# Projection tiles 4 to 27 in pairs, by seven block products in place of eight

## The reference, cut to what matters

```
u = h @ w_in                                   # 320 x 1024 @ 1024 x 14640, fp32
u_gate, u_gla, u_rwkv, u_ssm = _split(u, (N_GATE, GLA_PROJ, RWKV_PROJ, SSM_PROJ))
# RWKV rows are mixed with the row before them:
us = u + (full[:, :-1] - u) * mu
```

## Time and profile before

| what | value |
|---|---|
| median of 3 runs | 1505.06 us (1503.83 to 1506.8) |
| span of the profiled execution | 1502.1 us |
| PE busy | 1457.5 us, 97% |
| PEld busy | 1011.2 us, 67% |
| DVE, ACT, POOL busy | 647.1, 390.4, 116.8 us |
| granted TensorE clock, mean | 0.996 |

### The profile page before, as it was taken

The page is one execution under the profiler, slowest core; times in us unless marked ns, Lnnn a source line. Parts: engine busy times, 40 slices in busy tenths (PEclk is TensorE's granted clock), DMA queues, the critical chain, the costliest instruction groups (busy, mean ns, idle before and its releaser), DMA issues.

```text
span 1502.1 us, 31068 instructions
## 1 busy us (share of the span) xinstructions
PE 1457.5 (97%) x13071; PEld 1011.2 (67%) x13071; DVE 647.1 (43%) x1227; ACT 390.4 (26%) x874; POOL 116.8 (8%) x107
## 2 busy tenths in 40 slices
PE   7999999999999999999999999999999999999995
PEld 6776667677776777767766765766666767675751
DVE  5223778875644677734541114622211112121228
ACT  2112444442322554435431011111111111111111
POOL 3000113121010000000000000000000001000000
PEclk9999999999999999999999999999999999999998
DMA  7778375563344544565577538689999999999985
GB/s 243 168 174 181 101 214 166 132 203 97 103 130 147 138 112 116 178 180 163 135 231 263 157 100 359 251 337 399 417 423 430 428 426 429 426 428 429 427 342 211
DMA packets 157017, 375.27 MB, mean 250 GB/s; under 512 B 101708, under 2 KB 110300, under 8 KB 139216
## 3 DMA queue, kind: packets, MB, share of 16 engines
q1 hardware_dynamic: 123712, 341.35, 63.9%
q10 hardware_dynamic: 26592, 15.49, 3.5%
q0 software_dynamic: 6576, 16.48, 3.2%
HBM read 327.14 MB, written 51.95 MB: 252 GB/s over the span
## 4 chain that ended last, share of the span: by engine, by line
PE 82%; DVE 7%; DMA 4%; ACT 2%; DVEq 2%; issue 1%; SPq 1%; ACTq 1%; POOLq 0%
PE PS L576 27%; PE PS L1069 14%; PE PS L919 8%; PE PS L1036 7%; PE PS L1088 6%; PE PS L624 4%; PE PS L1041 2%; PE PS L957 2%; DVE region L1492 2%; DVE region L1499 2%; PE PS L632 1%; ACT L1172 1%; PE PS L1052 1%; PE PS L1077 1%; PE PS L817 1%
## 5 line engine op out<-in xcount | busy, mean ns | idle before, releaser
L576 PE MATMUL PS<-h0T,region 128*128 128x320 f32 x1808 | 510.2, 437 | 1.0 <-issue 0.8
L576 PEld LDWEIGHTS PS<-h0T,region 128*128 128x128 f32 x1808 | 336.8, 190 | 144.6 <-issue 12.2
L1172 ACT ACTIVATE region<-PS 128x9 f32<-128x9 f32 (+6 forms) x407 | 148.5, 383 | 681.9 <-PE PS L576 311.8
L1069 PE MATMUL PS<-region 128*64 128x512 f32 x1024 | 228.8, 592 | 0.0
L1069 PEld LDWEIGHTS PS<-region 128*64 128x64 f32 x1024 | 124.5, 137 | 92.2 <-issue 31.9
L1492 DVE TENSOR_TENSOR region<-region 128x256 f32<-128x256 f32 (+10 forms) x210 | 127.0, 624 | 96.8 <-ACTq L1218 76.2
L919 PE MATMUL PS<-region 128*128 128x320 f32 x512 | 138.6, 433 | 1.3 <-DMA region<-wo 1.2
L919 PEld LDWEIGHTS PS<-region 128*128 128x128 f32 x512 | 97.0, 190 | 42.5 <-issue 1.7
L1172 ACT ACT_TABLE_LOAD x80 | 102.6, 1283 | 73.1 <-DMA region<-projected 56.7
L1088 PE MATMUL PS<-region,history 128*64 128x512 f32 x512 | 119.7, 596 | 1.0 <-ACTq L1454 0.7
L1172 ACT ACTIVATE region<-region 128x256 f32<-128x256 f32 (+8 forms) x160 | 81.2, 531 | 147.9 <-DMA region<-projected 37.0
(11 more groups left out here) (210 smaller groups left out, 1163.8 us busy)
## 6 DMA issues: line engine op xcount, KB each, us to landing
region<-moe_w SPq DMA_DIRECT2D x64, 2048.0 KB, 17.4
region<-moe_w SPq DMA_DIRECT2D x64, 1024.0 KB, 15.0
region<-w_in SPq DMA_DIRECT2D x115, 512.0 KB, 5.6
region<-wo SPq DMA_DIRECT2D x32, 512.0 KB, 3.6
projected<-region ACTq DMA_DIRECT2D x65, 167.5 KB, 3.9
expert_rows<-region SPq DMA_DIRECT2D x20, 512.0 KB, 7.2
region<-expert_rows SPq DMA_DIRECT2D x5, 2048.0 KB, 14.4
region<-projected SPq DMA_DIRECT2D x10, 768.0 KB, 6.3
```

What stands on the lines that cost most here:

```text
L576: last = mm(PS[:, 6 + i % 2, 0:NTOK], WR[:, i, k, :], H0T[:, k, :], start=(k == 0), stop=(k == KT - 1))
L1069: last = mm(PS[tiles(i), 2, :], XE[:, k, tiles(i)], W13[r][i][:, k * 512:k * 512 + 512], start=(k == 0), stop=(k == KT - 1))
L1172: return nc.scalar.activation(out, in_, f, **kw)
```

## The change

Tiles 4 to 27 are computed two at a time. Two tiles are 256 features by 320 tokens over a width of 1024, which is cut into 2 x 2 x 2 blocks: feature tile a or b, the first or second half of the width (four blocks of 128 each), and the first or second 32 tokens of each chunk (`H0H[:, k, 0]` and `H0H[:, k, 1]`, 160 tokens each). Eight block products would be needed; the scheme takes seven, each of four matmuls with 160 moving columns, on sums and differences of blocks. Three PSUM banks (`X`, `Z`, `W`) hold them, two sets of three by turns.

- DVE makes four differences of token blocks once (`TSUM`), each 128 x 640, and adds the partial sums in PSUM onto staged parts, four `TENSOR_TENSOR` of 160 columns for a pair (`quads`).
- POOL makes four sums of weight blocks for every pair (`weight_sums`), each a `TENSOR_TENSOR` of 128 x 512, and one sixth of its old job after each of the pairs 1 to 6 (`keep_rows`).
- ACT copies four partial sums out of PSUM for a pair (`keep`), then the chunk edges (`edges`), and issues the stores of the pair before between its second and third `keep` (`tile_out`).
- PE signals `tile_done` for both tiles in its fifth product, since the last two products read only sums.
- SP's wait for `h_kept` goes; the scale and bias have moved. Three semaphores are shared under double names.

```diff
+            def project_pair(m, u):
+                pair, a, b = m * 2 + u - 2, 2 * u, 2 * u + 1
+                X, Z, W = (quad_sum(3 * u + x) for x in range(3))
+                def product(out, lhs, rhs, start, freed=False):
+                    for k in range(KH):
+                        last = mm(out, lhs(k), rhs(k), start=start and k == 0, stop=k == KH - 1, skip_group_check=True)
+                        if freed and k < 2:
+                            last.then_inc(sem("tile_done"), 1)
+                    last.then_inc(sem("quad"), 1)
+                for i in (a, b):
+                    pe.wait_ge(sem(f"weights_in{i}"), (m + 1) * 16)
+                pe.wait_ge(sem("quads_out"), pair + 1)
+                product(X, lambda k: WR[:, a, k, :], lambda k: H0H[:, k, 0], True)
+                product(Z, lambda k: WR[:, b, KH + k, :], lambda k: TSUM[:, 3, k], True)
+                pe.wait_ge(sem("weights_summed"), pair + 1)
+                pe.wait_ge(sem("quad_kept"), pair * 4 + 1)
+                product(X, lambda k: WSUM[u][:, 1, k], lambda k: TSUM[:, 1, k], False)
+                pe.wait_ge(sem("quad_kept"), pair * 4 + 2)
+                product(Z, lambda k: WR[:, a, KH + k, :], lambda k: H0H[:, KH + k, 0], True)
+                product(W, lambda k: WSUM[u][:, 0, k], lambda k: TSUM[:, 0, k], True, True)
+                pe.wait_ge(sem("quad_kept"), pair * 4 + 3)
+                product(X, lambda k: WSUM[u][:, 2, k], lambda k: TSUM[:, 2, k], False)
+                pe.wait_ge(sem("quad_kept"), pair * 4 + 4)
+                product(W, lambda k: WSUM[u][:, 3, k], lambda k: H0H[:, KH + k, 1], False)
...
+            pe.wait_ge(sem("token_sums"), 1)
             with pe.Fori(1, PRE // RING) as m:
-                for i in range(RING):
-                    project(m, i)
+                for u in range(2):
+                    project_pair(m, u)
...
+            for p in range(PAIRS):
...
+                act.wait_ge(sem("tile_mixed"), 2 * p + 2)
+                keep(p, 1, a, 0, X)
+                keep(p, 2, b, 0, Z)
+                if p > 0:
+                    for n in (RING + 2 * p - 2, RING + 2 * p - 1):
+                        tile_out(n)
+                keep(p, 3, a, 1, X)
+                keep(p, 5, b, 1, W)
+                act.wait_ge(sem("quads_out"), p + 3)
+                for n in (RING + 2 * p, RING + 2 * p + 1):
+                    edges(n)
+                act.drain().then_inc(sem("tile_moved"), 2)
...
+            def quads(p):
...
+                dve.wait_ge(sem("quad"), 7 * p + 4)
+                dve.wait_ge(sem("quad_kept"), 4 * p + 1)
+                tt(quad_out(a, 0), quad_out(a, 0), Z, add)
+                dve.wait_ge(sem("quad"), 7 * p + 6)
+                dve.wait_ge(sem("quad_kept"), 4 * p + 4)
+                for j in range(2):
+                    tt(quad_out(b, j), quad_out(b, j), X, add)
+                dve.wait_ge(sem("quad"), 7 * p + 7)
+                tt(quad_out(a, 1), quad_out(a, 1), W, add)
+                dve.drain().then_inc(sem("quads_out"), 1)
...
+            def weight_sums(p):
...
+                for i in (a, b):
+                    pool.wait_ge(sem(f"weights_in{i}"), (p // 2 + 2) * 16)
+                if p > 1:
+                    pool.wait_ge(sem("quad"), 7 * p - 7)
+                ptt(S1, A21, A22, add)
+                ptt(S3, A11, A21, sub)
                 pool.drain()
+                ptt(S2, S1, A11, sub)
+                pool.drain()
+                ptt(S4, A12, S2, sub)
+                pool.drain().then_inc(sem("weights_summed"), 1)
```

More of the change, by code:

```diff
@@ L175, in hybrid_layer, with quad_sum, quad_out @@
         assert at[0] <= REGION.shape[1], at[0]
+        tail = REGION[:, at[0]:at[0] + 2048]
+        assert at[0] + 2048 <= REGION.shape[1]
         LORA, G2 = (OT[:, 16:].rearrange("p a b -> p (a b)")[:, k * D:k * D + D] for k in range(2))
+        TSUM = shaped(OT[:, 8:16].rearrange("p a b -> p (a b)"), 4, KT // 2, NTOK // 2)
+        spare = OT[:, 16:].rearrange("p a b -> p (a b)")[:, 2 * D:]
+        WSUM = [shaped(v, 4, KT // 2, 128) for v in (spare[:, 0:2048], tail)]
+        H0H = H0T.rearrange("p k (c h w) -> p k h c w", c=NCH, h=2)
+        KH = KT // 2
+        def quad_sum(b):
+            return shaped(PS[:, b, 0:NTOK // 2], NCH, L // 2)
+        def quad_out(i, j):
+            return STG[:, i, :, HIST + 32 * j:HIST + 32 * j + 32]
         at[0] = mixer_base
@@ L1226, in move, with keep, edges @@
                 act.dma_start(ut[n, :, :, :], STG[:, i, :, :]).then_inc(sem(f"store_done{i}"), 16)
-            for n in range(PRE):
-                move(n // RING, n % RING)
+            def keep(p, made, i, j, region):
+                act.wait_ge(sem("quad"), 7 * p + made)
+                a_(quad_out(i, j), region, ACT.Copy)
+                act.drain().then_inc(sem("quad_kept"), 1)
+            def edges(n):
+                i = n % RING
+                act.wait_ge(sem(f"store_done{i}"), (n // RING + 1) * 16)
+                src = STG[:, i, :, HIST:CW]
+                a_(STG[:, i, 1:NPC, 0:HIST], src[:, 0:NPC - 1, L - HIST:L], ACT.Copy)
+                a_(STG[:, i, 0:NCH:NPC, 0:HIST], HISTS[:, n, :, :], ACT.Copy)
+                if n >= T_XBC:
+                    k = n - T_XBC
+                    a_(CVO[:, :, k, :], src[:, NPC - 1:NCH, L - HIST:L], ACT.Copy)
+                    a_(CV[:, i], src, ACT.Identity, scale=VEC[:, V_CW + 72 + k:V_CW + 73 + k], bias=VEC[:, V_CB + k:V_CB + k + 1])
+                elif n < T_MISC:
+                    a_(SHO[:, :, n], src[:, NPC - 1:NCH, L - 1], ACT.Copy)
@@ new lines, in tile_out @@
+            def tile_out(n):
+                i = n % RING
+                if n < T_MISC:
+                    act.wait_ge(sem("tile_mixed"), n + 1)
+                    act.dma_start(ut[n, :, :, HIST:CW], CV[:, i]).then_inc(sem(f"store_done{i}"), 16)
+                elif n < T_XBC:
+                    act.wait_ge(sem("tile_moved"), n + 3)
+                    act.dma_start(ut[n, :, :, :], STG[:, i, :, :]).then_inc(sem(f"store_done{i}"), 16)
+            for n in range(RING):
+                move(n // RING, n % RING)
@@ new lines, in _ @@
+            for p in range(PAIRS):
+                u, a, b = p % 2, 2 * (p % 2), 2 * (p % 2) + 1
+                act.wait_ge(sem("tile_mixed"), 2 * p + 2)
+                X, Z, W = (quad_sum(3 * u + x) for x in range(3))
+                keep(p, 1, a, 0, X)
[9 more added lines that the diff above has]
+                act.drain().then_inc(sem("tile_moved"), 2)
@@ L1230, in _ @@
+            for n in range(PRE - 2, PRE):
+                tile_out(n)
             meet(act, 1)
@@ L1565, in _ @@
                 dve.drain().then_inc(sem("h0T_ready"), 1)
+            dve.wait_ge(sem("h0T_ready"), EVICTED)
+            for out, x, y in ((0, H0H[:, 0:KH, 1], H0H[:, 0:KH, 0]), (2, H0H[:, KH:, 1], H0H[:, 0:KH, 1]),
+                              (1, H0H[:, KH:, 1], TSUM[:, 0]), (3, H0H[:, KH:, 0], TSUM[:, 1])):
+                tt(TSUM[:, out].rearrange("p k (c w) -> p k c w", c=NCH), x, y if out in (0, 2) else
+                   y.rearrange("p k (c w) -> p k c w", c=NCH), sub)
+                dve.drain()
+            nc.vector.sem_inc(sem("token_sums"), 1)
+            nc.vector.sem_inc(sem("quads_out"), 2)
             dve.wait_ge(sem("vectors_in"), 32)
```

62 lines of the change are left out of this document (39 added, 23 removed).

## The result

The changed kernel takes 1518.14 us, the median of four runs (1515.05 to 1523.61), against 1505.12 us before: a ratio of 1.0098 with a 95% interval of 1.0074 to 1.0122, slower by about 1% (the two medians alone give 1.0087). The prediction was 1522.7 us, within 1500 to 1531. The profiled execution has a span of 1517.3 us, 15.2 more than the one before.

A forecast was written before the change was run, and what follows sets the result against it. PE's columns were taken as the bound. Tiles 4 to 27 were to take 118.6 us against 103.4 (+15.2), the end +2.4: +17.6 on a median of 1505.1 gives 1522.7 us, range 1500 to 1531.

The forecast's parts named there:

- PE's passes: Tiles 4 to 27: 160-column passes at 0.137 us, 7.67 us a pair, 92.1 us for twelve pairs, gaining 11.3 us.
- The lock of POOL on DVE: DVE's two mixing operations, beside POOL's sums, wait for POOL's operation under way: 1.2 us or more on average.
- The place: PE waits about 2.5 us in each pair at its sixth product, put down to ACT.
- The sum of the stretch: Tile 4 to end of tile 27: 8.9, 61.2 and 48.5 us make 118.6 us against 103.4, +15.2.
- The end of the stretch: After tile 27: the mixer's first product waits for rows fetched after tile 25's later store, +2.4 us.
- locked pair: A pair whose loop is held by POOL's sums lying on DVE's mixing: 10.0 to 10.8 us.
- half locked: Rival: weights land at 7.5 to 8.3 us, loops alternate between 7.7 and 11.9 us; 1511 us; chance 0.17.
- the forecast case: Sums hold the mixing in tiles 4 to 27 throughout: 1514 to 1531 us; chance 0.55.
- The free case: Rival: sums miss the mixing in tiles 4 to 27, the loop stays free; 8.1 us less, 1497 us; chance 0.20.
- theory A: Follow-up forecasts: POOL slows DVE's mixing, delaying ACT's copies for PE; with both stores last, 1498 to 1503 us.

The follow-up runs named there:

- quiet POOL: Changed kernel with POOL's weight sums made for the first two pairs only and no scaling of kept rows: 1500.52 us, ratio 0.9980 to the kernel before.
- the kernel before with sums: Kernel before the change plus 48 extra POOL sums of 128x512, four for every two tiles: 1504.76 us, ratio 1.0001.
- both stores last: Changed kernel with ACT issuing both stores of the pair before behind the third and fourth copies: 1516.31 us, ratio 1.0080 to the kernel before.
- split stores: Changed kernel with ACT's order third copy, store of tile a, fourth copy, store of tile b: 1519.12 us, ratio 1.0091 to the kernel before.
- waiting sums: Changed kernel without kept-row scaling, POOL's sums waiting until the pair two before is mixed: 1509.12 us, ratio 1.0037 to the kernel before.
- four edits: Changed kernel with stores split between copies, sums waiting for mixing, row scaling four pieces first and two last, SP's second fetch later: 1521.17 us, ratio 1.0111.
- pieces at both ends: Changed kernel with row scaling three pieces first and three last, token differences after tile 0's mixing, sums waiting for mixing, both SP fetches later: 1512.32 us, ratio 1.0070.

## Why the prediction was right, step by step

- **PE's passes.** Predicted 0.137 us a pass; two products of eight start 34.35 and 35.44: 0.136. 672 passes make 91.4 us, against 92.1 predicted. Right.
- **The lock of POOL on DVE.** Predicted 1.2 us or more on average for mixing; measured 0.91 and 1.08, as not every operation met a sum. The quiet POOL shows that this is the cause of nearly all of the loss (16 us), and the kernel before with sums shows that it costs only through the loop.
- **The place.** Predicted at the sixth product, put down to ACT. Of eight waits for ACT one is at the third product of pair 0 (2.03 us, 38.72), the others at sixth products, in seven of the twelve pairs, 0.94 to 3.49 us long and 1.8 on average where 2.5 in each pair was forecast. Right in place, too large in size.
- **The sum of the stretch.** Predicted 118.6 us, measured 115.9, but by other terms, so that the agreement is in part luck. Waits were predicted as 26.5 us in all. They are 16.1, and where POOL's work hardly met the mixing the pair ran free (pairs 5, 9 and 10 have no wait). The difference is made up by a term that I had set to nothing: the half clock after gaps. Products 3 to 7 of pair 0 took 7.22 us instead of 5.43, two products of pair 1 3.76 instead of 2.17, two of pair 6 and the one behind them 6.10 instead of 3.26: 6.2 us. I wrote that the clock stays at 1.00, from the earlier trace rows, which hold no gap; that was no ground for it. The remaining 2 us lie in the restarts (the first eight passes after a wait take 1.19 us instead of 1.09) and hand-overs.
- **The end of the stretch.** Predicted +2.4 us, measured +1.6, and not by the way that was forecast. The forecast let tile 28's wait for the last edges hide in a longer wait of the mixer for rows that are fetched late. The rows came in time: the store of tile 25 was issued by 146.2, sooner than in a locked pair, and from tile 28 to the mixer's first product it takes 9.43 us in both kernels. What is left is tile 28's wait, 1.74 us where it was 0.25:

```profile
152.13 8.85 PE L593 MATMUL PS<-h0T,region 128*128 128x320 f32 x32 [1.74 <-ACTq L1319]
161.56 1.16 PE L690 MATMUL PS<-region 64*64 64x64 f32 x64 [0.57 <-ACTq L1332]
```

- **The rival "half locked"** (1511 us) describes the alternation better than the forecast case does; with the 6.2 us of the clock on top it comes to 1517, near the 1518 measured. The free case failed in part where it was said to, by the pieces of the old job; without them half of the loss was still there (6.9 us of 13.0). Its price, 8.1 us less, was too good: with POOL quiet the mixer's first product comes 5.7 us earlier, and the kernel is 3 us faster.

What stays open: after the mixer's first product, identical code takes 1354.9 us in the profile before, 1361.2 in the profile of the kernel before with sums (which is its slowest run, 1510.09; the median is unchanged) and 1355.6 to 1361.6 in the changed kernels. For the same 12526 matmul passes PE is busy 1320.5 us before and 1326.5 with the sums, 1326.5 with both stores last and 1326.6 with split stores: the passes themselves took longer, at a mean granted clock of 0.99 against 1.00. In the kernel before with sums 4.0 us of it lie within one chunk of the RWKV mixer, from 197.40 to 219.83, where before it took from 197.54 to 215.98. A wait of PE was longer there, and eight passes of 320 columns behind it took 4.63 us instead of 2.42 (the granted clock is 0.50 from 203.03 to 208.23, against 1.00 before). The kernel before, then the kernel before with sums:

```profile
202.08 0.46 PE L624 MATMUL PS<-region 64*64 64x64 f32 x16 [1.57 <-issue]
202.47 2.42 PE L576 MATMUL PS<-h0T,region 128*128 128x320 f32 x8
...
203.03 0.71 PE L625 MATMUL PS<-region 64*64 64x64 f32 x16 [2.67 <-issue]
203.66 4.63 PE L577 MATMUL PS<-h0T,region 128*128 128x320 f32 x8
```

So most of the 4.0 us is the clock again. Why the wait was 1.1 us longer was not found, nor what sets off such slow spells; they are why arrivals at the mixer and the times of these profiles differ by some us. Open too is why the repairs fell short: theory A's forecasts of the time were missed in the runs with both stores last, split stores, waiting sums, four edits and pieces at both ends, each by 7 us or more. The experiments show what the meeting of POOL and DVE costs in this kernel, and no way to keep POOL's sums and be rid of that cost.

## What to carry to other kernels

A saving in one engine's arithmetic that needs sums and copies on three others must be priced by the loop through all of them, not by each one's busy share: here POOL and DVE each had half their time idle and their meeting cost about 16 us. Look at which copy stands behind which wait in an in-order queue, and follow a removed wait to its next place: moving the stores away gave PE 9 us, and 4 of them went back at the next fetch. An engine that is slowed off the critical path costs nothing until an order ties it in, as the kernel before with sums shows.

## What the runs showed of the hardware

After some waits of PE its granted clock was half. After idle times of 2.61 us (pair 1, 54.14) and 3.49 us (pair 6, 102.73) eight passes took 2.50 us instead of 1.35; after 1.90 us (65.38), 1.12 and 0.94 us they took 1.35, and the clock stayed at 1.00. After 2.03 us (pair 0, 38.72) the first eight took 1.35 as well, but the eight behind them 2.17 instead of 1.25, and the granted clock of 38.72 to 45.94 was 0.76. The length of the wait alone does not settle it: with split stores the same place in pair 0 waited 2.58 us, and the clock stayed at 1.00 (40.09 to 46.00); with POOL quiet it waited 2.33 us, also without loss.

```profile
40.09 1.35 PE L607 MATMUL PS<-region 128*128 128x160 f32 x8 [2.58 <-ACTq L1277]
```

Where the clock fell, the slow passes cost 0.6 to 0.9 of the gap itself (1.8 us after 2.03, 1.6 after 2.61, 2.8 after 3.49).

An operation of DVE with two SBUF inputs gets through between two of POOL's, and DVE waits for the whole rest of POOL's. POOL loses less by it: of its four sums the second, which follows the first with nothing between, took 1.51 or 1.52 us instead of 1.27 in seven of the twelve pairs; the third and fourth, which wait for the one before to be finished, took 1.34 at most but for one (1.50). The Trainium skill, "SBUF — State Buffer", section "Who interferes with whom", has it that a DVE instruction with two SBUF inputs contends with a GpSimd instruction that reads SBUF, and calls the shared ports an exclusive lock. The trace agrees for DVE; POOL lost at most half of the 0.49 to 0.55 us that the DVE operation takes alone.
